# The second norm's scale and offset as single rows, spread over the partitions by TensorE

## The reference

```python
for i in range(DEPTH):                      # DEPTH = 2
    ...
    x = layer_norm(DEEPNORM_ALPHA * x + mixed, ln1_g[i], ln1_b[i])
    ffn = moe_ffn(x.reshape(B_ * S_, D), w_router[i], ...)   # sum of 6 gated experts + a shared expert
    x = layer_norm(DEEPNORM_ALPHA * x + ffn, ln2_g[i], ln2_b[i])

def layer_norm(x, g, b):
    ...
    return ((xf - mu) * lax.rsqrt(var + LN_EPS) * g + b).astype(x.dtype)
```

## Time and profile before

| what | value |
|---|---|
| median of 3 runs | 1962.59 us |
| lowest and highest | 1956.61 and 1962.62 us |
| the profiled execution's own time | 1963.41 us |
| its span on the engines | 1961.6 us |
| mean granted TensorE clock | 0.978 |
| PE busy | 1791.5 us, 91% |
| DVE, ACT, POOL busy | 751.8, 379.8, 353.6 us |

### The profile page before, as it was taken

One profiled execution on the slowest core, in us unless ns is written; L12 is line 12 of the kernel. 1 busy time (PEld: TensorE's weight loads), 2 busy tenths in 40 slices (PEclk: granted clock), 3 DMA queues, 4 the chain that ended last, 5 costly groups with the idle time before them and its releaser, 6 DMA issues. The chain is left out here.

```text
span 1961.6 us, 36107 instructions
## 1 busy us (share of the span) xinstructions
PE 1791.5 (91%) x12636; PEld 1110.6 (57%) x12637; DVE 751.8 (38%) x2180; ACT 379.8 (19%) x870; POOL 353.6 (18%) x450
## 2 busy tenths in 40 slices
PE   9999999899998989878999979999879999997877
PEld 7888445456665545543444458755446666664442
DVE  4222754623333222225155654426523333332225
ACT  2111741011111111102354143201001111110001
POOL 8442000111111111110013632100111111111110
PEclk9999999999999999999999979899989999999999
DMA  6220234699999999998213220208898999999997
GB/s 232 78 79 23 97 125 182 252 414 421 422 421 421 421 421 421 421 415 310 65 54 87 54 43 2 88 1 318 332 409 354 422 421 421 420 421 423 421 416 302
DMA packets 144184, 541.80 MB, mean 276 GB/s; under 512 B 31030, under 2 KB 68498, under 8 KB 94302
## 3 DMA queue, kind: packets, MB, share of 16 engines
q1 hardware_dynamic: 122782, 490.20, 62.4%
q0 software_dynamic: 21312, 50.37, 6.6%
HBM read 521.58 MB, written 46.14 MB: 289 GB/s over the span
## 5 line engine op out<-in xcount | busy, mean ns | idle before, releaser
L723 PE MATMUL bank<-W,XT 128*64 128x256 f32 x2880 | 330.7, 387 | 40.6 <-DMA W<-in_w_exp_gate_dram 17.8
L723 PEld LDWEIGHTS bank<-W,XT 128*64 128x64 f32 x2880 | 235.5, 140 | 146.1 <-DMA W<-in_w_exp_gate_dram 29.0
L760 PE MATMUL bank<-W,ht 128*64 128x512 f32 x720 | 166.0, 602 | 13.5 <-DMA W<-in_w_exp_down_dram 8.9
L2265 PE MATMUL bank<-XT,room 128*128 128x512 f32 x352 | 159.9, 609 | 0.0
L734 DVE TENSOR_TENSOR sig<-sig,bank 128x256 f32<-128x256 f32 x72 | 30.3, 421 | 274.8 <-ACT sig L730 274.7
L723 PE MATMUL bank<-room,XT 128*64 128x256 f32 x864 | 102.8, 391 | 16.1 <-DMA room<-in_w_exp_gate_dram 8.4
L2265 PEld LDWEIGHTS bank<-XT,room 128*128 128x128 f32 x352 | 66.7, 194 | 83.0 <-issue 82.7
L736 DVE TENSOR_TENSOR h<-sig,bank 128x256 f32<-128x256 f32 x72 | 30.3, 421 | 216.6 <-PE bank L723 216.6
L789 POOL DMA_INDIRECT y_rows<-y,row x36 | 36.6, 1018 | 421.8 <-DVE y L782 421.8
L789 POOL DMA_INDIRECT y_rows<-XT,row x36 | 36.3, 1008 | 419.2 <-DVE XT L782 419.2
L709 ACT ACTIVATE XT<-bank 128x512 f32<-128x512 f32 x74 | 44.2, 597 | 330.4 <-PE bank L701 330.4
(11 more groups left out here) (491 smaller groups left out, 2774.2 us busy)
## 6 DMA issues: line engine op xcount, KB each, us to landing
W<-in_w_exp_gate_dram SPq DMA_DIRECT2D x88, 1024.0 KB, 25.6
W<-in_w_exp_up_dram SPq DMA_DIRECT2D x88, 1024.0 KB, 27.0
W<-in_w_exp_down_dram SPq DMA_DIRECT2D x88, 1024.0 KB, 26.6
room<-in_w_exp_gate_dram SPq DMA_DIRECT2D x40, 1024.0 KB, 24.2
third_high<-in_w_exp_down_dram SPq DMA_DIRECT2D x40, 1024.0 KB
W<-y_rows SPq DMA_DIRECT2D x24, 1024.0 KB, 13.5
third_up<-in_w_exp_up_dram SPq DMA_DIRECT2D x20, 1024.0 KB, 27.8
w_shg<-in_w_exp_up_dram SPq DMA_DIRECT2D x20, 1024.0 KB, 25.3
```

The lines of the kernel that those rows point to most:

```text
L723: last = pe.matmul((gate, up)[m][64 * a:64 * a + 64, :], xt[s][:, k, 64 * a:64 * a + 64], weights(w, a, m)[:, k * FE:(k + 1) * FE], start= ...
L760: last = pe.matmul(B[5 + half][64 * a:64 * a + 64, :], ht[:, j, 64 * a:64 * a + 64], weights(w, a, 2)[:, at:at + 512], start=(j == 0), sto ...
L2265: last = pe.matmul(main(i)[:], wc[i % WBUFS][:, kb, :], K.XT[:, kb, :], start=(kb == 0), stop=(kb == KD - 1))
```

## The change

The two vectors are no longer broadcast by DMA. SyncE loads each as one row of 4 KB into partition 0 (`vector_rows`, in the free up weights of slot 2, printed as `third_up`), ahead of the shared down weights. Behind the product (1,2) TensorE multiplies a row of ones (1 x 128) by each of the four parts of 512 columns, into banks 4 to 7, which the tiles 2 and 3 use afterwards. ScalarE copies the four banks to where the vectors stood before, `third_high`; its copies stand between the diagonals of (1,2) and those of (2,0). TensorE waits for the fourth copy before the shared product of tile 2, and VectorE waits for it, instead of the loads, before L1118 of tile 0. Both layers do this.

```diff
@@ Combination.__init__
+        self.vector_rows = shared.high[0:1, 0:2 * D]
+        self.vectors_spread, self.vectors_kept = sem("vectors_spread"), sem("vectors_kept")
+        self.vectors = room[:, 0, :]
         self.ln = LayerNorm(K, scope, f"ln2_{L}", K.in_["ln2_g"][L:L + 1, :], K.in_["ln2_b"][L:L + 1, :],
-                            room[:, 0, :])
+                            self.vectors)
+        self.ln.ready = (self.vectors_kept, 4)
@@
     def load_early(self, sp):
+        for i, src in enumerate(self.ln.src):
+            sp.dma_start(self.vector_rows[:, i * D:(i + 1) * D], src).then_inc(self.ln.loaded, 16)
         self.shared.load_down(sp, self.down_room)
-        self.ln.load(sp)
@@ products
         self.row_product(pe, 0, 2)
         self.row_product(pe, 1, 2)
+        self.spread_vectors(pe)
+        pe.wait_ge(self.vectors_kept, 4)
         self.shared_product(pe, 2)
@@
+    def spread_vectors(self, pe):
+        K = self.K
+        pe.wait_ge(self.ln.loaded, 32)
+        for i in range(4):
+            pe.matmul(K.banks[4 + i][:], K.ones[0:1, :], self.vector_rows[:, i * 512:(i + 1) * 512],
+                      start=True, stop=True).then_inc(self.vectors_spread, 1)
+
+    def keep_vectors(self, act):
+        for i in range(4):
+            act.wait_ge(self.vectors_spread, i + 1)
+            act.activation(self.vectors[:, i * 512:(i + 1) * 512], self.K.banks[4 + i][:], ACT.Copy).then_inc(self.vectors_kept, 1)
@@ scale
             for h in range(2):
                 act.activation(self.diagonal[:, n, h, :], self.two, ACT.Copy,
                                scale=self.gates[:, h, t, q:q + 1]).then_inc(self.diagonals, 1)
+            if n == 2 * ROW_PAIRS - 1:
+                self.keep_vectors(act)
@@ LayerNorm.normalize
         if t == 0:
-            dve.wait_ge(self.loaded, 32)
+            dve.wait_ge(*(self.ready or (self.loaded, 32)))
```

More of the change, by code:

```diff
@@ L1099, in __init__ @@
         self.done = scope.sem(f"{name}_done")
+        self.ready = None
     def load(self, eng):
```

## The result

| | before | changed |
|---|---|---|
| median (6 runs each) | 1962.61 us | 1972.76 us |
| lowest, highest | 1956.61, 1963.59 | 1970.30, 1975.82 |
| ratio, 95% interval | | 1.0058, 1.0043 to 1.0072 |
| the profiled execution, its span | 1963.41, 1961.6 us | 1970.61, 1968.9 us |

The change makes the kernel slower by 10.2 us in the medians, clear of its interval; 6.2 were forecast, and the measured time lies near the upper end of the range given. The profiled execution of the changed kernel is one of its quickest, and its own difference, 7.2 us, is less than what its two changed places cost. So I compare the places first.

What follows compares the result with a forecast made beforehand. TensorE alone was taken to set the end from (1,2) on. Added work of 9.0 us less 2.8 us of relief gave +6.2 us on 1962.59, so 1968.8 us; range 1962.0 to 1973.4.

Steps and rivals of the forecast that it cites:

- The relief of the queue: SyncE's loads, each layer: 1 MB less saves 2.5 us; waits before (0,0) and (0,1) go, 1.13 and 1.09 us.
- I take 6.0 us, which is 1.5 us earlier: Last scatter before (1,2): lands after 6.0 us instead of 7.46, so 2.8 us come back over both layers.
- the first rival: Last scatter's landing doesn't move, so nothing comes back before (1,2): +9.0 us, 1971.6; chance 0.20.
- The stall: TensorE between (1,2) and tile 2's shared product: calls 3.5, hops and fourth copy 1.0, together 4.5 us a layer.
- So the number of rows doesn't matter: Added one-row products on TensorE: priced like a shared product's four calls, 3.63 us with the switch; 3.5 taken.
- ScalarE and VectorE behind the copies: Diagonals, table load and root move behind the copies; VectorE's 2.68 us slack goes, TensorE still bounds by 0.1; cost 0.
- S: Start of the added calls on TensorE; fourth copy ends 4.2 us later, TensorE goes on 4.5 us later.
- the two signs: Forecast wrong if TensorE waits over 1 us before (1,2) in both layers, or VectorE still 2 us before tile 3.
- I let its delay through in full: End of layer 0: one chain through the transposes follows, so its whole delay was counted in the kernel's time.
- the range: Kernel time 1962.0 to 1973.4: from +1.2 less 2 for the runs' scatter to +9.6 and 1 more.

Runs made afterwards that it cites:

- the repetition: The changed kernel run once more, unaltered: 1972.67 us beside 1962.07 for the kernel before, ratio 1.0057.
- e2: Kernel before with four idle products over one row added between (1,2) and the shared product of tile 2, both layers: 1967.81 us, ratio 1.0033.
- e5: Changed kernel with its four one-row spreading products put ahead of (1,2): 1966.97 us, ratio 1.0014 to the kernel before.
- e1: Changed kernel with each spreading product contracting over all 128 partitions instead of one: 1965.63 us against 1961.01 for the kernel before, ratio 1.0021.
- e6: Changed kernel with the spreading products ahead of (1,2) and contracting over 128 rows: 1961.82 us, ratio 1.0001 to the kernel before.
- e3: Kernel before with four idle products over all 128 rows between (1,2) and the shared product of tile 2: 1966.02 us, ratio 1.0023.
- e7: Kernel before with the shared product of tile 2 moved ahead of (1,2): 1961.85 us against 1962.07, ratio 0.999.
- e11: Kernel before with the two broadcasts issued behind the first four loads of rows: 1961.56 us, ratio 0.9998.
- e10: Kernel before with another 1 MB load queued behind the two broadcasts: 1968.28 us against 1961.21, ratio 1.003.

## Why the forecast was too low, step by step

- **The relief of the queue: right.** 1 MB less brought (0,0) and (0,1) without a wait in every run that had it.
- **"I take 6.0 us, which is 1.5 us earlier": wrong.** The last scatter lands after 7.3 to 8.1 us whatever stands in SyncE's queue. What came back is read off the start of (1,2) after the shared product of tile 0: from 18.5 to 18.1 us in layer 0 and from 17.8 to 17.2 in layer 1, 1.1 us together where 2.8 were taken (the repetition: -0.2 and 1.2). It is the first rival's mechanism. The rule that I had set against the step, from "DMA: Bandwidth & Descriptors" of the Trainium skill, section "Queues, rings and completion order", that the engines take turns between queues, is the one with which the constant landing agrees (7.3 to 8.1 us); no run shows the turns themselves.
- **The stall: right in size in layer 0.** 4.39 us against 4.5: 3.70 for the products (3.5), and 0.69 for the fourth copy with its hops, for which I had put 1.0.
- **"So the number of rows doesn't matter": the step that failed most.** It is right for the duration of a call (3.70 us for the four calls, with 1, 32 or 128 rows) and wrong for what follows. Behind products over one row the clock is granted at its lower level, in the changed kernel with 1.7 us (5.33 - 3.63) in layer 0, and in layer 1 with 2.3 in the shared product and 0.65 in the spread, which the fall reached (5.04 us for the stall instead of 4.39). That is 4.7 us of the 6.1 by which 12.3 exceed the forecast's 6.2; the relief that didn't come is another 1.7, and the stall itself, twice 4.39 where 4.5 was taken, gives 0.2 back. No term for the clock stood in the sum, in the range or among the rivals, and the row of calls over 8 partitions was looked at for its duration alone. It could not have shown it: these calls come eight at a time and take 1.15 us, and the clock beside them, from 991 to 1079 us, is 1.00. What a spread over a number of rows between 1 and 32 would do, no run tells.
- **ScalarE and VectorE behind the copies: right, and never the bound.** The root of tile 0 starts at S + 8.5 us in layer 0 (916.56 - 908.04), forecast 8.4. VectorE was to work without a pause up to tile 3 in layer 1; it waits 2.20 us there, because the clock's fall delayed TensorE by 3.0 us more than reckoned (VectorE starts tile 3 at 1958.70, 24.55 us after the start of the spread, where TensorE was to offer it after 21.6). A wait of 2 us at this place was one of the two signs that I had named of a wrong forecast, and it is there. The other, waits of over 1 us before (1,2) in both layers, came in layer 0 alone (1.86, and 0.62 in layer 1).
- **"I let its delay through in full": not so in one execution.** The profiled execution entered the end of layer 1 only 0.5 us later than before (1915.09 against 1914.60) though layer 0's end had cost 5.6. TensorE's timeline at one pass of layer 1 tells where the rest is. Of before:

```profile
1467.05 10.11 PE L723 MATMUL bank<-W,XT 128*64 128x256 f32 x64 [4.68 <-issue]
```

and of the changed kernel:

```profile
1470.26 7.13 PE L723 MATMUL bank<-W,XT 128*64 128x256 f32 x64 [1.23 <-issue]
```

The stall ahead of these weights is 3.5 us shorter, and the products behind it have the full clock, 3.0 us less. The repetition has a stall of 4.11 us at this pass and 8.63 for the products, so this belongs to the execution and not to the kernel. The stall is as short in the runs with idle products over 128 and 32 rows (0.97 and 0.94 us), and 4.1 to 5.2 us in all others whose layer 1 can be read. What makes it, for which the profile names no releaser, stays open.

The forecast of "slower" holds, and its 6.2 us were too few against 10.2 measured. By the stretches the changed places cost 12.3 and 13.7 us in two executions; that the medians show 10.2 and 10.6 leaves some 2 to 3 us that are given back elsewhere or lie in the scatter of the runs. The other runs with products added have such a rest too: 11.6 us in the stretches against 6.8 in the median (e2), 10.5 against 4.9 (e5), 9.7 against 4.6 (e1), 4.0 against -0.3 (e6), 6.3 against 5.0 (e3). From the shared product of tile 3 in layer 0 to that of tile 0 in layer 1 TensorE took 997.5 us in the kernel before and 988 to 996 in these kernels; but it took 997.7 and 990.2 in two kernels without added products (e7, e11), whose stretches are within 1.4 us of those before. So a part may be given back there as a rule, and no run here tells how much. What a microsecond in a stretch costs the kernel is therefore not shown; what the place costs, and why, is.

The measured time lies in the stated range, but the range had no term for the clock. Its top is the stall without any relief, 9.6 us, and 1 more; the changed places went beyond that, and the rest named above brought the time back into it. That is luck. (By their own terms the range's ends are 1961.8 and 1973.2 us, 0.2 lower than stated.)

## What to carry to other kernels

A product used as a broadcast costs its columns, however few rows it contracts over, and here more than its columns: over one row it brought the clock down for the full products behind it. If it must be done on TensorE, let it contract over all partitions with a one-hot column as weights (the other partitions then count as zeros), put it where the engine waits anyway, and put its evacuation beside other products.

When a wait at the head of a chain is taken away, look for the next event that the chain can't pass. Here that was a scatter whose landing stayed within 7.3 to 8.1 us in every run, and three waits that were to vanish became one. A landing time should only be moved in a forecast if two places of the trace with different load in front of it show it moving.

## What the runs showed of the hardware that was not expected

The granted clock fell from 2.4 to 1.2 GHz without any gap in TensorE's work: in the run with idle one-row products the engine is busy 3.60 of 3.60 us and the stretch behind it has a mean of 0.68; eight places of eight with one row, none of two with 32 rows, none of five with 128 where the clock was up before (e1 in layer 1, e3 and e6 in both). In two places it fell behind waits instead, of 2.07 (e1, layer 0) and 2.93 us (e10, layer 1), with products over all 128 rows on both sides. "TensorE: Matmul & The Clock Gate" in the Trainium skill, "Part 1: The HAM clock gate", ties the clock to how busy TensorE has been and speaks of gaps; by the engine's records this one was busy, so here the page doesn't cover what the measurement shows, and the measurement decides.

What an issue takes on SyncE did not go by its own size. The first behind the last expert's weights, a row of 4 KB, took 4.74 us in layer 0 and 1.54 in layer 1; in the kernel before the 1 MB of down weights stood in its place and took 4.56 and 3.26, and behind the two rows the same down weights took 0.41 and 0.55. It cost nothing here, since SyncE was to wait anyway.
